# A transformer block on one core: bias table in eight transfers, the first tile in halves, the last square on TensorE, raw queries on ScalarE, a block-ordered end

## The reference, cut to what matters

```python
n = rmsnorm(h, norm_mix)
qa, ka, va, qb, kb, vb, ga, gb = split(n @ w_in)
y_a = differential_attention(qa, ka, va, lam, ...)      # rope on qa and ka
y_b = neighbourhood_attention(qb, kb, vb, na_rpb)       # adds a bias table
merged = sigmoid(ga) * (y_a @ w_proj_a) + sigmoid(gb) * (y_b @ w_proj_b)
h = h + merged @ w_out
xn = rmsnorm(h, norm_ffn)
# peer_ffn: 8 heads x 2 key sets; query = xn @ w_query, s = query . sub_keys
#   top 16 of each set, top 16 of their sums, softmax g
#   a = gelu(xn . expert_u[idx]);  out = sum g * a * expert_v[idx]
h = h + peer_ffn(xn, w_query, sub_keys, expert_u, expert_v)
out = rmsnorm(h, norm_final)
```

## Time and profile before

| | us |
|---|---|
| median of three runs | 1021.07 |
| the profiled execution's own time | 1022.16 |
| its span, first to last instruction | 1020.3 |
| TensorE busy | 1005.3 |
| VectorE busy | 855.6 |
| ScalarE busy | 599.9 |
| GpSimd busy | 82.0 |

### The profile page before, as it was taken

How to read it: one execution, slowest core, us unless ns; L and a number is a source line. 1 busy time by engine, 2 the same in 40 slices (tenths; PEclk the granted TensorE clock), 3 DMA queues, 4 the chain that set the end, 5 groups by cost and what they waited for, 6 DMA issues and landing times.

```text
span 1020.3 us, 20502 instructions
## 1 busy us (share of the span) xinstructions
PE 1005.3 (99%) x6942; PEld 926.2 (91%) x6942; DVE 855.6 (84%) x1681; ACT 599.9 (59%) x1109; POOL 82.0 (8%) x38
## 2 busy tenths in 40 slices
PE   9899999999999999999999999999999999999997
PEld 9889899989999999999999999988888888888885
DVE  6888868789999989999999999777777777777775
ACT  6356544634545468888888888555554544445453
POOL 0000000157790000000000000000000000000000
PEclk9999999999999999999999999999999999999999
DMA  8644445636477766666666666797777777777771
GB/s 300 218 134 138 128 140 170 227 123 224 158 245 224 242 216 207 208 208 204 213 208 210 197 218 210 255 324 236 233 232 234 230 235 237 236 231 240 233 231 67
DMA packets 86597, 214.93 MB, mean 211 GB/s; under 512 B 9600, under 2 KB 42752, under 8 KB 86016
## 3 DMA queue, kind: packets, MB, share of 16 engines
q1 hardware_dynamic: 86240, 213.46, 64.5%
q10 hardware_dynamic: 288, 0.53, 0.1%
HBM read 195.08 MB, written 18.87 MB: 210 GB/s over the span
## 4 chain that ended last, share of the span: by engine, by line
PE 92%; DVE 5%; DMA 1%; ACT 1%; issue 1%; DVEq 0%; SPq 0%
PE pO L1105 33%; PE pO L1336 18%; PE pTT L1361 17%; PE pM L1361 17%; PE pTT L1310 1%; PE pSS L1310 1%; DMA raw<-in_stream 1%; PE pSS L1166 1%; DVE wlos L666 1%; PE pM L1203 1%; DVE gates L689 1%; DVE xlo L695 1%; PE pTT L1185 0%; PE pSS L1279 0%; PE pM L1197 0%
## 5 line engine op out<-in xcount | busy, mean ns | idle before, releaser
L457 ACT ACTIVATE whis<-raw 128x1024 fp32r<-128x1024 f32 x328 | 345.1, 1053 | 50.8 <-PE pO L1105 36.9
L666 DVE TENSOR_TENSOR wlos<-raw,whis 128x1024 fp32r<-128x1024 f32 x170 | 206.3, 1219 | 21.0 <-ACT whis L457 20.7
L1105 PE MATMUL pO<-xhi,whis 128*128 128x256 f32 x760 | 214.3, 282 | 1.8 <-ACT qkT L502 1.0
L1105 PE MATMUL pO<-xlo,whis 128*128 128x256 f32 x760 | 212.2, 279 | 0.0
L1105 PE MATMUL pO<-xhi,wlos 128*128 128x256 f32 x760 | 212.0, 279 | 0.0
L1021 DVE TENSOR_TENSOR wlos<-raw,whis 128x1024 fp32r<-128x1024 f32 x125 | 153.2, 1226 | 64.6 <-ACT whis L457 64.6
L616 ACT ACTIVATE ghi<-wfull 128x256 fp32r<-128x256 f32 x128 | 53.8, 420 | 171.2 <-PE pM L1361 171.2
L1105 PEld LDWEIGHTS pO<-xhi,whis 128*128 128x128 f32 x760 | 142.7, 188 | 3.2 <-issue 1.9
L1336 PE MATMUL pO<-xlo,whis 128*128 128x256 f32 x512 | 143.4, 280 | 0.0
L1336 PE MATMUL pO<-xhi,wlos 128*128 128x256 f32 x512 | 143.0, 279 | 0.0
L1336 PE MATMUL pO<-xhi,whis 128*128 128x256 f32 x512 | 143.0, 279 | 0.0
(11 more groups left out here) (218 smaller groups left out, 1892.1 us busy)
## 6 DMA issues: line engine op xcount, KB each, us to landing
raw<-in_stream SPq DMA_DIRECT2D x200, 512.0 KB, 3.7
raw<-in_vrows SPq DMA_DIRECT2D x128, 512.0 KB, 3.5
a_scratch<-ast SPq DMA_DIRECT2D x128, 128.0 KB, 1.8
aring<-a_scratch SPq DMA_DIRECT2D x128, 128.0 KB, 3.3
biasm<-in_bias SPq DMA_DIRECT2D x1, 2048.0 KB, 10.7
keysT<-in_keys SPq DMA_DIRECT2D x1, 1024.0 KB, 5.5
h_scratch<-h1tok SPq DMA_DIRECT2D x1, 1024.0 KB, 6.3
htok<-h_scratch SPq DMA_DIRECT2D x1, 1024.0 KB, 8.1
```

What stands on the lines that cost most here:

```text
L457: act.activation(whi[s], raw[s][:], ACT.Copy).then_inc(hi_ready, 1)
L666: dve.tensor_tensor(wlo[t % RING], raw[t % RING][:], whi[t % RING].bitcast(F32), ALU.subtract).then_inc(lo_ready, 1)
L1105: last = pe.matmul(dst, st, mv, start=(c == 0 and q == 0), stop=(c == len(terms) - 1 and q == 2))
```

## The change

Six edits. The bias table comes in eight transfers of 256 KB, each behind the load of one of the tiles 8 to 15. Each rope is cut in two: the tables, the shuffle and the first product at steps 5 and 9, the second product and the sum at steps 6 and 10; each part stands behind that step's low part. Tile 0 is loaded in two halves, VectorE makes both its parts, the x parts change queues, there are 12 warm-up matmuls instead of 17, and TensorE takes tiles 0 and 1 together in a new order (`two_tiles`). VectorE adds one square less; TensorE multiplies the eighth by ones itself. ScalarE copies the queries out of PSUM unscaled, and the scores of each token are scaled by rstd when ScalarE takes them, in two instructions instead of one; two transposes bring rstd to the token side. At the last projection tile VectorE writes `mlo` before the next low part instead of behind it. In the value stage `ghi` and `glo` become rings of four, and the last three tiles are processed piece by piece: five pieces of 512, 512, 512, 256 and 256 columns, each over all three tiles; the last two go to banks of their own, and the old accumulator is added beforehand. The gain is multiplied in before the norm is known, and both the last scaling and the stores are shared by VectorE and ScalarE.

```diff
-ROPE_AT = {6: 0, 10: 1}
+ROPE_AT = {5: (0, 0), 6: (0, 1), 9: (1, 0), 10: (1, 1)}
-WARM = 17
+WARM = 12
...
-            sp.dma_start(raw[0][:], stream[0]).then_inc(raw_landed[0], 16)
-            load_x(1)
+            sp.dma_start(raw[0][:, 0:HALF, :], stream[0, :, 0:HALF, :]).then_inc(head_landed, 16)
+            sp.dma_start(raw[0][:, HALF:C, :], stream[0, :, HALF:C, :]).then_inc(raw_landed[0], 16)
+            load_x(2)
...
-            for t in range(RAW, 2 * RAW):
+            for t in range(RAW, 4 * RAW):
                 load(t, t % RAW, stream[t])
-            sp.dma_start(biasm[:], bias).then_inc(bias_landed, 16)
+                if t >= 2 * RAW:
+                    part = t - 2 * RAW
+                    at = (slice(None), part // 4, slice(part % 4 * 2, part % 4 * 2 + 2))
+                    sp.dma_start(biasm[at], bias[at]).then_inc(bias_landed, 16)
...
-            low_w(0)
+            for half in range(2):
+                dve.wait_ge(raw_landed[0] if half else head_landed, 16)
+                part = slice(half * HALF, (half + 1) * HALF)
+                dve.tensor_copy(whi[0][:, part], raw[0][:, part]).then_inc(head_hi, 1)
+                dve.wait_ge(head_hi, half + 1)
+                dve.tensor_tensor(wlo[0][:, part], raw[0][:, part], whi[0][:, part].bitcast(F32), ALU.subtract).then_inc(lo_ready if half else head_lo, 1)
...
             for k in range(T_QUERY, T_U):
+                j = k - T_QUERY
                 hi_at(k + LEAD)
-                if k == T_QUERY:
+                act.wait_ge(tile_done, k + 1)
+                act.activation(qp[:, j, :], pO[k % 2][:, 0:T], ACT.Copy).then_inc(evac_act, 1)
+                if j == 0:
                     rms_root(2)
...
-                if c == C - 1:
+                if c == C - 2:
                     ins.then_inc(squares_added, 1)
...
-            add_square(C - 1)
...
-                dve.tensor_tensor(qp[:, j, :], pO[k % 2][:, 0:T], rstd[:], ALU.mult).then_inc(evac_dve, 1)
...
-                pe.matmul(bank[:, 0:T], ones[:], gates[:, 0, :], start=True, stop=True).then_inc(ssq_done, 1)
+                ins = pe.matmul(bank[:, 0:T], ones[:], gates[:, 0, :], start=True, stop=k == 1)
+                if k == 2:
+                    pe.wait_ge(squares, C + 1)
+                    ins = pe.matmul(bank[:, 0:T], ones[:], gates[:, C - 1, :], start=False, stop=True)
+                ins.then_inc(ssq_done, 1)
...
+            def v_last_tiles():
+                for j, (b, lo, hi) in enumerate(PIECES):
+                    last = None
+                    for i in range(NE_TILES - BY_BLOCK, NE_TILES):
+                        if (b, lo) == (0, 0):
+                            v_wait(i)
+                        for n, (st, mv) in v_terms(i % RING, b):
+                            last = pe.matmul(ends[j], st, mv[:, lo:hi], start=hi - lo < 512 and i == NE_TILES - BY_BLOCK and n == 0,
+                                             stop=i == NE_TILES - 1 and n == 2)
+                    last.then_inc(acc_done, 1)
...
+            def rows_scaled(b, hi, inverse):
+                dve.wait_ge(fin_inverse, b + 1)
+                dve.wait_ge(gained_out, 5 if b else 2)
+                dve.tensor_scalar(rows[b][:, 0:hi], rows[b][:, 0:hi], inverse, None, ALU.mult).then_inc(out_ready, 1)
```

More of the change, by code:

```diff
@@ L242, in build @@
             wfull = [sbs(vphase, f"wfull{s}", [P, T]) for s in range(2)]
-            ghi = [sbs(vphase, f"ghi{s}", [P, T], F32R) for s in range(2)]
+            ghi = [sbs(vphase, f"ghi{s}", [P, T], F32R) for s in range(2)] + ghi_more
+        rows = [raw[s][:].rearrange("p c n -> p (c n)") for s in range(TB)]
         def K(name):
@@ L429, in _ @@
                     load_a(g * RAW + s, s)
[L430 removed]
+            for j, (b, lo, hi) in enumerate(((0, 0, 512), (1, 0, BY_DVE))):
                 sp.wait_ge(out_ready, j + 1)
[L432 to L434 removed]
+                sp.dma_start(out[:, b, lo:hi], rows[b][:, lo:hi]).then_inc(out_stored, 16)
+            sp.wait_ge(out_stored, 16 * 4)
         @block.gpsimd
@@ L1087, in _ @@
             residual(2)
-            whole_sum(0)
+            rows_scaled(0, 512, fin[:, 7:8])
             residual(3)
-            inverse(0)
-            rows_out(0)
-            whole_sum(1)
-            rows_out(1)
-            inverse(1)
-            rows_out(2)
-            rows_out(3)
+            gained(2)
+            residual(4)
+            dve.wait_ge(fin_sum, 4)
+            link(dve.scalar_tensor_tensor(fin[:, 11:12], fin[:, 2:3], D * EPS, fin[:, 3:4], ALU.add, ALU.add))
+            dve.tensor_scalar(fin[:, 8:9], fin[:, 11:12], 1.0 / D, None, ALU.mult).then_inc(fin_ms, 1)
@@ L1290, in _ @@
                     square_sum(pM[0], 2)
+                if j == 2:
+                    pe.wait_ge(rstd_ready, 2)
+                    for b in range(TB):
+                        last = pe.transpose(pM[1][:, b * P:(b + 1) * P], rstd[:, b * P:(b + 1) * P], ident)
+                    last.then_inc(rstd_turned, 1)
                 if j >= 2:
@@ L1354, in v_tile @@
                 last = None
                 for b in range(TB):
-                    wh, wl = ghi[s % 2][:, b * P:(b + 1) * P], glo[s % 2][:, b * P:(b + 1) * P]
-                    terms = list(enumerate(((wh, vh), (wh, vl), (wl, vh))))
-                    steps = [(n, t, q) for q in range(2) for n, t in terms] if final else [(n, t, q) for n, t in terms for q in range(2)]
-                    for n, (st, mv), q in steps:
-                        last = pe.matmul(acc[b][q], st, mv[:, q * 512:(q + 1) * 512], start=first and n == 0, stop=final and n == 2)
-                        if final and n == 2:
-                            last.then_inc(acc_done, 1)
@@ L1364, in v_tile @@
-                if not final:
-                    last.then_inc(tile_done, 1)
+                    for n, (st, mv) in v_terms(s, b):
+                        for q in range(2):
+                            last = pe.matmul(acc[b][q], st, mv[:, q * 512:(q + 1) * 512], start=first and n == 0, stop=n == 2 and (b, q) == closed)
+                last.then_inc(tile_done, 1)
+            def v_last_tiles():
[3 more added lines that the diff above has]
+                        if (b, lo) == (0, 0):
+                            v_wait(i)
+                        for n, (st, mv) in v_terms(i % RING, b):
+                            last = pe.matmul(ends[j], st, mv[:, lo:hi], start=hi - lo < 512 and i == NE_TILES - BY_BLOCK and n == 0,
+                                             stop=i == NE_TILES - 1 and n == 2)
+                    last.then_inc(acc_done, 1)
```

225 lines of the change are left out of this document (152 added, 73 removed).

## The result

| | before | after |
|---|---|---|
| median, us | 1020.0 (1018.04 to 1022.18, 5 runs) | 1012.86 (1012.52 to 1013.17, 5 runs) |
| the profiled execution's own time | 1022.16 | 1012.58 |
| its span | 1020.3 | 1010.7 |

The changed kernel takes 0.993 of the time before, 95% interval 0.9912 to 0.9947: faster, by 7.1 us between the medians and by 9.6 between the two profiled executions. The forecast was 1011.6, in a range of 1009.3 to 1016.0.

A forecast was written before the change was run, and what follows sets the result against it. TensorE, busy 1005.3 of 1020.3 us, bounds the kernel; only its waits, low clock and the ends count. 3.7 + 0.3 + 3.8 + 0.4 + 1.3 = 9.5 us less: 1012.7 for the profiled execution, 1011.6 from the median; range 1009.3 to 1016.0.

The forecast's parts named there:

- Front, 3.7: From the start to the first scores: these begin at 47.7 instead of 51.41, 3.7 us less (bounds 2.2 and 5.9).
- The second of the new waits: Before the first scores: TensorE waits for VectorE's low and rope parts from 46.3, 1.3 us.
- The first, "1.2 to 1.6": At the pair after tile 7: TensorE waits 1.2 to 1.6 us for tile 9's low part, behind the rope's first part.
- the low clock at the new wait: Rival, front: the wait for tile 9's low part brings a fall of clock costing about 1.5 us, 1013.1; chance 0.14.
- Loads still late: Rival, front: 768 KB a tile is too much, waits stay in another form, front gives only 0.5, 1014.8; chance 0.06.
- VectorE's lead: At the start, tile 0 in halves: VectorE's list runs 0.55 us ahead (bounds 0 and 1.2).
- `mlo`, 0.3: At the last projection tile: writing `mlo` before the low part removes a 0.3 us wait, 0.3 less.
- The last square, 3.8: Before the query stage: TensorE sums the last square, 4.0 us less, transposes cost 0.2; 3.8 less (bounds 0 and 4.3).
- The race: Near 205 us: VectorE's last but one sum and GpSimd's low part start 0.11 us apart; the 3.8 hangs on it.
- Queries, 0.4: Query stage: ScalarE copies raw queries, 16 products leave VectorE, the 0.4 us wait for `qp` goes; 0.4 less.
- The slower rival: Query stage: ScalarE's list delays weight copies, VectorE instructions meet GpSimd; 1027.1 if all 16 stretch; chance 0.04.
- Tail, 1.3: Last residual to end: 2.4 us instead of 3.92, 1.5 gained, 0.2 given back for the store; 1.3 less (0.6 to 1.8).

The follow-up runs named there:

- the small operation: The changed kernel with one VectorE copy of a 128 x 1 column added ahead of the last sum of squares left on VectorE: 1015.71 us, ratio 0.9966.

## Why the prediction was right, and where not

**The whole.** 9.5 us were forecast against the profiled execution and 9.6 came. The median went down by only 7.1, and by 6.6 against the 36 other runs of before. The step that was off is the last of the sum, "taken from the median, 1011.6": it subtracts the fall of the clock behind both waits, which the profiled execution had, from a median whose runs, by their mean clock, mostly had less of it. Of the 1.3 us between 1011.6 and 1012.86, 1.1 are this; for the profiled execution the working had 1012.7. Between the fastest executions of both kernels 1016.1 - 1010.7 = 5.4 are left (spans). Profile against profile the gain is 3.9 at the first scores (forecast 3.7), 213.83 - 205.85 = 8.0 behind the tile that follows the sum by ones (4.1 more; forecast 0.3 + 3.8), 1013.67 - 1005.39 = 8.3 at the last residual (0.3 more; forecast 0.4) and 9.6 at the end (1.3 more; forecast 1.3). That every term comes out so near is in part luck: 3.2 of these us are low clock, which this execution of before happened to have behind both waits.

**Front, 3.7.** The scores came at 47.52 where 47.7 was forecast, and the pair at 32.21 where 32.2 was. The second of the new waits, before the scores, was 1.4 where 1.3 was forecast. The first, "1.2 to 1.6", was 0.4: it was sized by a TensorE that is 1.2 ahead by tile 6, and it was some 0.5 ahead. The place was right, the size was not, and the clock stayed at 1.00, so *the low clock at the new wait* did not come. *Loads still late* did not come either: the bias parts land in 5.4 us at the median of eight. What was wrong is whose merit the 3.7 is. The ropes over two slots give nothing here (1012.5 without them), and cost 2.0 where the bias is late. The bias parts give 2.2 to 3.9, the halves of tile 0 0.7 where 0.55 was forecast as VectorE's lead.

**`mlo`, 0.3.** The wait is gone from the list; it was not tried alone.

**The last square, 3.8.** The mechanism was right in each step: 4.06 was forecast from the end of the tile to the end of the next, and 201.48 to 205.85 is 4.37, against 8.06 before: 3.7. This is so with the fall of the earlier trace rows; it is worth 2.4 at the median of the runs with the sum back on VectorE, 2.0 to 2.4 in the group of the profiled run, where the clock did not fall. The term was mis-sized by taking one execution's clock for the rule. The race was closer than the 0.11 of before: 0.06. The rule of the Trainium skill in "SBUF — State Buffer", section "Who interferes with whom", said what the runs then showed from both sides: 0.41 when the sum is first, 0.44 when GpSimd is held back, and 2.46 or 2.57 when the sum is second.

**Queries, 0.4.** Between the two profiles 0.3; undone by itself 1.5, of which 1.05 lie within the span. The forecast priced the removed wait for `qp` (0.5 in the experiment) and not what 16 instructions less on VectorE, and the later place of the normed x, do to its meetings with GpSimd. The slower rival looked at the same place and found it harmless; stretched rows are there in the changed kernel too (2.54 for one, 2.27 for two together), but VectorE has 26.4 busy us in the 36 from 200 on instead of 31.8 with the products, and TensorE waits for none.

**Tail, 1.3.** From the profile 3.92 - 2.15 = 1.77 gained and 0.5 given back in the last store, 1.3; the experiment has 1.1. The working had 1.5 and 0.2.

**The slower rival.** It did not happen: no wait for `whis` or GpSimd between 200 and 260. Its price has a small slip: 25 - 9.8 is 15.2 and not 15.5.

**The rings of four** for `ghi` and `glo` had no term; no wait of TensorE for them is left in the list above, and they were not tried alone.

Still open is whether the spread of the kernel before has a further cause; the 3.2 us at one mean clock speak for it. That its spans follow the mean clock was seen in 36 runs, and the stretch of low clock itself in one profile of before and two of the experiments.

## What to carry to other kernels

Before a median is charged with the low clock of one profile, look whether runs of the same kernel differ by as much as the fall would cost: here a wait of 2.2 to 2.4 us cost its own length in some runs and over half as much again in others. Where two engines' instructions shut each other out, write down the margin of their starts; at 0.06 us a copy of one column costs 2.9 us, and a wait that fixes the order cost nothing. And look for idle time of the engine that is late next: here the split of the ropes gave nothing until its parts were moved into 2.2 idle us, and then 1.3 to 1.6. Last, compare the spans beside the times: one variant lost 0.4 us outside its span, which no view of the trace shows.

## What the runs showed of the hardware

A wait of TensorE of 2.4 us was followed by a tile at granted clock 1.00 (2.82 us, the sum back on VectorE) and, in the kernel before, by one at 0.54 (3.67 us). A wait of 2.2 was followed by 1.00 too (the small operation), one of 2.3 by 0.50 (before); waits of 2.5 and 2.8 were followed by a fall in both experiments that have them, waits up to 1.5 in none of the profiles. When VectorE's sum of 256 columns began 0.06 us ahead of GpSimd's part, the sum took 0.41 and the part 2.58; with the part 0.06 ahead, the sum took 2.57 and the part 2.35; kept apart, 0.44 and 2.39. A VectorE product with one operand in PSUM took 0.41 us while GpSimd worked, between two that took 1.98 and 2.29.
